# Input projection of a transformer layer: seven half-width products in place of eight, and the cache copies begun with the last column block

## What is computed

```
h  = rmsnorm(x, g_attn_norm)                  # 320 tokens x 2048
q, kc, vc, ks, vs, kw, vw, gt, u, v = split(h @ w_in)      # 2048 x 4656
q_rot, ks, kw = partial_rope(q), partial_rope(ks), partial_rope(kw)
gates = sigmoid(gt);  u = gelu(u);  v = rmsnorm(gelu(v), g_sgu_v)
kc_all, vc_all = compress(cached and new kc, vc; w_cmp_*1, w_cmp_*2, pe_cmp_*)
win_k_s = concat(cache_win_k, kw)[:, -wb:]    # and win_v_s: mostly a copy of the cache
mk, mv = rmsnorm(mem, g_mem_src) @ (w_mem_k, w_mem_v)
```

## Time and profile before

| | us |
|---|---|
| median of 3 runs (1652.16 to 1656.22) | 1654.53 |
| the profiled execution | 1652.59 |
| its span | 1650.8 |
| projection phase, first product to the next phase's first instruction | 80.58 to 424.04 |

### The profile page before, as it was taken

How to read it: one execution, slowest core, us unless ns; L and a number is a source line. 1 busy time by engine, 2 the same in 40 slices (tenths; PEclk the granted TensorE clock), 3 DMA queues, 4 the chain that set the end, 5 groups by cost and what they waited for, 6 DMA issues and landing times. The chain is left out here.

```text
span 1650.8 us, 19858 instructions
## 1 busy us (share of the span) xinstructions
PE 1443.3 (87%) x7384; PEld 794.2 (48%) x7385; DVE 387.3 (23%) x972; ACT 296.7 (18%) x667; POOL 83.5 (5%) x111
## 2 busy tenths in 40 slices
PE   7999999999999988878899999859879978699890
PEld 4444445556788756644444575533323333233330
DVE  3101010000365265466310212521100100101015
ACT  3000000011333234357100113201000000000001
POOL 0000000000200000000000000001001010010100
PEclk9999999999999689979899999969989988899895
DMA  9276224252242077500943222979998999979975
GB/s 357 104 303 254 103 99 139 99 173 103 103 153 65 22 220 229 158 12 1 340 135 110 94 102 103 388 276 401 392 415 307 414 404 388 416 309 414 414 299 195
DMA packets 112657, 371.89 MB, mean 225 GB/s; under 512 B 17331, under 2 KB 55259, under 8 KB 82919
## 3 DMA queue, kind: packets, MB, share of 16 engines
q1 hardware_dynamic: 106898, 334.88, 53.5%
q0 software_dynamic: 5552, 27.89, 4.9%
q10 hardware_dynamic: 144, 8.26, 1.2%
HBM read 394.60 MB, written 26.49 MB: 255 GB/s over the span
## 5 line engine op out<-in xcount | busy, mean ns | idle before, releaser
L2359 PE MATMUL bank<-ring,hT_e 128*64 x576 | 251.7, 595 | 8.2 <-DMA ring<-in_w_exp_up 6.8
L2360 PE MATMUL bank<-ring,hT_e 128*64 128x512 f32 x576 | 251.9, 595 | 0.0
L2376 PE MATMUL bank<-W,const 128*64 128x512 f32 x576 | 150.2, 677 | 53.1 <-DMA W<-in_w_exp_down 48.6
L2359 PEld LDWEIGHTS bank<-ring,hT_e 128*64 128x64 f32 x576 | 78.5, 138 | 167.7 <-issue 167.7
L490 PE MATMUL bank<-raw,hT 128*128 128x512 f32 (+1 forms) x320 | 131.6, 573 | 0.6 <-PEq L243 0.6
L490 PE MATMUL bank<-w_in,hT 128*128 128x512 f32 (+2 forms) x320 | 123.7, 547 | 0.0
L2376 PEld LDWEIGHTS bank<-W,const 128*64 128x64 f32 x576 | 45.0, 155 | 145.0 <-issue 100.5
L1715 PE MATMUL bank<-W,mixT 128*128 128x512 f32 x256 | 113.4, 603 | 1.6 <-DVE mixT L1950 1.6
L490 PEld LDWEIGHTS bank<-raw,hT 128*128 128x128 f32 x320 | 61.5, 193 | 67.5 <-issue 67.3
L490 PEld LDWEIGHTS bank<-w_in,hT 128*128 128x128 f32 x320 | 60.4, 190 | 61.0 <-issue 61.0
L1715 PEld LDWEIGHTS bank<-W,mixT 128*128 128x128 f32 x256 | 49.0, 193 | 63.5 <-issue 61.4
(11 more groups left out here) (403 smaller groups left out, 1782.5 us busy)
## 6 DMA issues: line engine op xcount, KB each, us to landing
ring<-in_w_exp_gate SPq DMA_DIRECT2D x80, 1024.0 KB
ring<-in_w_exp_up SPq DMA_DIRECT2D x72, 1024.0 KB
W<-in_w_exp_down SPq DMA_DIRECT2D x72, 1024.0 KB
raw<-in_w_in SPq DMA_DIRECT2D x3, 4096.0 KB
W<-in_w_out SPq DMA_DIRECT2D x3, 4096.0 KB, 13.3
w_in<-in_w_in SPq DMA_DIRECT2D x2, 4096.0 KB, 14.7
k_in<-in_cache_sel_k SPq DMA_DIRECT2D x64, 128.0 KB
v_in<-in_cache_sel_v SPq DMA_DIRECT2D x64, 128.0 KB, 3.5
```

The lines of the kernel that those rows point to most:

```text
L2359: pe.matmul(bank[4 + u][0:NS, :], hT[:, u, c, :], w_g[:, c, :], start=(c == 0), stop=(c == KC - 1))
L2360: mm = pe.matmul(bank[4 + u][UP, :], hT[:, u, c, :], w_u[:, c, :], start=(c == 0), stop=(c == KC - 1))
L2376: mm = pe.matmul(bank[2 * u + n // 2][lane, :], actT[:, q, :], w_d[:, q, 512 * n:512 * n + 512], start=(q == 0), stop=(q == 3))
```

## The change

- The 256 prompt tokens are taken as two tiles, the 2048 rows as two halves, the columns of a block as two halves, and the 2 x 2 x 2 products of halves become seven, each of eight matmuls 128 tokens by half the width. Four sums of token blocks are made once (`sum_tokens`), four sums of weight halves for each block (`sum_weights`, DVE, into the memory of `w_in1`). ACT keeps four partial results for a block, DVE adds up four outputs (`add_up`). The sample tokens are multiplied as before (`THIRD`).
- Nine column blocks: five of 512, and `V1, UV, GU, U1` of 524. One weight buffer, loaded in two halves of rows (`load_in`).
- The memory keys' transposes stand ahead of block `Q0`.
- The compression's weights are loaded after the last block's; `pe_terms` and `pe_sums` follow the last block; the gather starts after product 3 of the last block; ACT issues the cache copies at the start of its work on the last block.
- 0.8 MB of constants (the memory of the kept partial results) is loaded at the start of the compression phase instead of at the start.

```diff
+            Q0, KS, Q1, KW, KC_, V1, UV, GU, U1 = range(9)
...
+            JOBS = {FIRST: m_jobs, KS: q_jobs(0), KW: q_jobs(1), KC_: k_jobs}
+            THIRD, P1, P2, P5, P6, P3, P7, P4 = range(1, 9)
...
+                    def load(n):
+                        sp.wait_ge(ready, made(n - 1, P1))
+                        sp.wait_ge(w_summed, added(n - 1, T3))
+                        load_in(sp, 0, *COLS[n])
+                        sp.wait_ge(ready, made(n - 1, P3))
+                        sp.wait_ge(w_summed, added(n - 1, T4))
+                        load_in(sp, 1, *COLS[n])
...
-                        if n == V1:
+                        if n == U1:
+                            sp.wait_ge(v_squared, TILES)
                             for u, kind in enumerate("kv"):
                                 sp.dma_start(w1[:, u, :, :], A[f"w_cmp_{kind}1"][0].rearrange("(m p) h -> p m h", p=P)).then_inc(cw_loaded, 16)
...
-                    pool.wait_ge(ready[0], TILES * (NT_IN // 2))
+                    pool.wait_ge(ready, made(NT_IN - 1, P3))
+                    pool.wait_ge(w_summed, added(NT_IN - 1, T4))
                     for turn in range(2):
                         gather_cmp(pool, turn)
...
+                        def product(to, left, right, start=True):
+                            for c in range(8):
+                                mm = pe.matmul(to, left(c), right(c), start=(start and c == 0), stop=(c == 7), skip_group_check=True)
+                            mm.then_inc(ready, 1)
...
+                        pe.wait_ge(kept, copied_out(n, K_THIRD))
+                        pe.wait_ge(w_summed, added(n, T1))
+                        product(b, lambda c: s1[:, c // 4, c % 4, :], lambda c: w_sum[:, 0, c, 0:half])
+                        pe.wait_ge(kept, copied_out(n, K_P1))
+                        pe.wait_ge(w_summed, added(n, T2))
+                        product(a, lambda c: s2[:, c // 4, c % 4, :], lambda c: w_sum[:, 1, c, 0:half], start=False)
...
+                    turn_blocks(FIRST)
                     for n in range(NT_IN):
                         multiply(n)
                         turn_blocks(n)
-                        if n == UV:
-                            pe_terms()
-                        if n == GU:
-                            pe_sums()
+                    pe_terms()
+                    pe_sums()
                     pe_columns()
...
                 def _(act):
                     own = act_steps.on(act)
                     act.wait_ge(blank_q, 2)
-                    act.wait_ge(ready[0], 1)
-                    for cache, dst in (("cache_win_k", "win_k_s"), ("cache_win_v", "win_v_s")):
...
+                    copy_jobs(act, act.copy, 0, FIRST)
+                    for n in range(NT_IN):
+                        if n == U1:
+                            for cache, dst in (("cache_win_k", "win_k_s"), ("cache_win_v", "win_v_s")):
+                                act.dma_start(out[dst][0, :, 0:WIN - NT].rearrange("b (s t) g d -> b s (t g d)", s=NT),
+                                              A[cache][0, :, NT:WIN].rearrange("b (s t) g d -> b s (t g d)", s=NT)).then_inc(window_out, 16)
+                        take(n)
+                        if n == GU:
+                            act.wait_ge(v_scaled, 1)
+                            act.activation(vms[:, :], vms[:, :], ACT.Sqrt).then_inc(v_rooted, 1)
+                        if n > KC_:
+                            finish(n)
                         copy_jobs(act, act.copy, 0, n)
...
+                        dve.tensor_tensor(t(0), part(0, 1), part(0, 0), ALU.subtract).then_inc(w_summed, 1)
...
+                        if n:
+                            dve.wait_ge(ready, made(n - 1, P4))
+                        dve.wait_ge(w_summed, added(n, T2))
+                        dve.tensor_tensor(t(3), t(1), part(1, 0), ALU.subtract).then_inc(w_summed, 1)
...
+                    for n in range(NT_IN):
+                        sum_weights(n)
+                        if 1 <= n <= KC_ + 1:
+                            take(n - 1)
+                        if n - 1 in JOBS and n - 1 != FIRST:
+                            copy_jobs(dve, dve.tensor_copy, 1, n - 1)
...
+                        add_up(n)
```

More of the change, by code:

```diff
@@ L263, in _ @@
                     sp.wait_ge(mem_made, 2)
[L264 removed]
+                    for v in range(2):
+                        load_in(sp, v, 0, 512)
                     sp.wait_ge(const_loaded, 16 * 5)
@@ L478, in multiply @@
                         half = width // 2
-                        pe.wait_ge(loaded[u], n // 2 * 16 + 16)
-                        if n >= 2:
[L481 to L493, removed]
-                                    mm = pe.matmul(bank[4 * u + r][64 * h:64 * h + 64, 0:half], hT[:, c, r * P:r * P + NS], part,
-                                                   start=(c == 0), stop=(c == KC - 1))
-                            mm.then_inc(ready[u], 1)
@@ new lines, in multiply @@
+                        for c in range(KC):
+                            if c % 8 == 0:
+                                pe.wait_ge(w_in_loaded[c // 8], 16 * n + 16)
+                            for h in range(2):
+                                mm = pe.matmul(b[64 * h:64 * h + 64, :], hT[:, c, 2 * P:2 * P + NS], w[:, c, h * half:(h + 1) * half],
+                                               start=(c == 0), stop=(c == KC - 1))
+                        mm.then_inc(ready, 1)
+                        if n >= 2:
+                            pe.wait_ge(kept, copied_out(n - 2, K_U3))
@@ L565, in _ @@
-                    for n in range(NT_IN):
-                        take(n)
+                        u, width = n % 2, COLS[n][1]
+                        half = width // 2
+                        a, b = (bank[4 * u + k][:, 0:half] for k in range(2))
+                        gelu = n > KC_ and n != GU
+                        act.wait_ge(ready, made(n, THIRD))
+                        if n == Q1:
+                            act.wait_ge(turned, J_BEFORE[KS + 1])
+                            act.wait_ge(roped, KS + 1)
@@ new lines, in take @@
+                        for h in range(2):
+                            to, shaped = half_of(n, 2, h)
+                            of = shaped(b[64 * h:64 * h + 64, :])
+                            ins = act.activation(to, of, ACT.Gelu_apprx_tanh) if gelu else act.copy(to, of)
+                        ins.then_inc(kept, 1)
+                        act.wait_ge(ready, made(n, P1))
+                        if n:
+                            act.wait_ge(summed, added(n - 1, C21))
+                        act.copy(kept_p1[:, 0:half], a).then_inc(kept, 1)
```

242 lines of the change are left out of this document (156 added, 86 removed).

## The result

The changed kernel takes **1669.48 us** (median of 8 runs, 1663.97 to 1672.76) against 1654.2 us (8 runs, 1652.16 to 1658.32): a ratio of 1.0089, 95% interval 1.007 to 1.0108. It is slower by 15 us. The profiled execution has a span of 1668.2 us, 17.4 more than before.

What follows compares the result with a forecast made beforehand. PE's own work was taken to set the phase's time, plus whatever makes PE wait. Terms gave -9.8 us, then +28 for the copies and +2 for the clock: +20.2, 1672.8 profiled, 1674 forecast, range 1664 to 1683.

Steps and rivals of the forecast that it cites:

- forecast case: Whole kernel: slower at 1674 us, range 1664 to 1683, the new last wait outweighing the phase's gain; chance 0.68.
- Products: PE's column blocks: seven 256-column products instead of eight half products, blocks of 31.4 and 32.2 us, saving 30.6 us.
- rival 3: Late halves: six blocks wait up to 0.8 us each for weights, 5 us in all, total 1679; chance 0.05.
- Turns: After KS and KW, transposes wait behind DVE's weight sums: 14.6 us each; with the memory's transposes, +17.0 us together.
- Clock: PE standing some 10 us twice: 2.8 us charged for each, less the 2.8 that goes: +2.8 us.
- Tail without the wait: Last block's end to next phase: 10.1 us, with DVE's output and copy ahead of the sums adding 1.0.
- Copies: Before `pe_terms`: cache copies hold up the compression's weights, so PE stands 28 us, 22 to 33.
- Sums at the low clock: After the last wait, PE's small sums start at the low clock: +2 us, 0 to 2.8.
- Rival 1: Weights get through in the gaps, only the gather is late: +11 us, total 1655, no change; chance 0.14.
- Rival 2: Copies do not hold other queues: no wait before `pe_terms`, -9.8 us, 1644, faster; chance 0.13.

Runs made afterwards that it cites:

- order experiment: Changed kernel, but after blocks KS and KW DVE rotates and copies the transposed jobs out before making the four weight sums: 1654.79 us, ratio 0.9989.
- sixteen-part run: Changed kernel with each cache copy written with an outer dimension of 16 instead of 8, same bytes, place and issue time: 1660.41 us, ratio 1.0023.
- the kernel with the new order, the weights first and sixteen parts: Changed kernel, DVE rotating and copying before its weight sums after KS and KW, compression's weights issued before the last half load, copies in sixteen parts: 1626.99 us, ratio 0.9827.

## Why the prediction was right

The forecast case came in: 1674 was predicted, 1669.5 measured, in the range of 1664 to 1683 that the case had for itself, and the wait that it named is the one that decides. By its own steps, in us of the profiled execution:

- **Products:** blocks of 31.4 and 32.2 predicted, 31.43 and 32.18 measured. The saving of 30.6 stands. No block starts late, so rival 3 falls.
- **Turns:** 14.6 each predicted, 15.1 measured; +7.8 and +9.05 instead of +7.3 and +8.6. PE stood for 10.65, ended by the copy into `qrT`, as written. With the 1.0 for the memory's transposes: +17.8 against +17.0. The order experiment shows the cause.
- **Clock:** +2.8 predicted, +0.4 measured (1.94 and 1.30 lost, 2.8 no longer). The step was wrong in taking 2.8 us for each stand; see the last section.
- **Tail without the wait:** 10.1 predicted, 10.2 in the five kernels without a wait there.
- **Copies:** 28 predicted (22 to 33), 24.6 measured. The mechanism is shown by the two directions of it: away from the copies the wait is gone (27.3 us between the last block and the next phase); put beside anything else (the first blocks' weights, the gather of the kernel before) they stall that by 24 and 12 us. The order of events is the predicted one, copies, gather, weights: the semaphore was reckoned for S+59 and came at S+56.8 (426.87), and the remaining 1.2 of the 3.4 too many is that 28 was taken where the count gave E+26.8. I had read the one-for-one from 8 packets; it holds in the finer rows above (8 beside 8) and in the sixteen-part run (96 beside 95). It is not the whole: from 382 to 384.5 SP's queue passed 80 packets beside 8 of the copies', 72 of them under 512 bytes, and again from 389.5 to 392 and from 394.5 to 397. Why the small ones go in bursts no run shows.
- **Sums at the low clock:** +2 predicted, +2.7 measured (9.81 against 7.15).
- **Rival 1** was hidden under the forecast: without the weights' wait the gather's costs 11.8. **Rival 2** did not come in: the copies went out before the weights were through, at S+0.7, a little ahead of the S+1 to S+5.4 reckoned.

These terms sum to -30.6 + 17.8 + 0.4 + 1.0 + 24.6 + 2.7 = +15.9, where the phase grew by 15.7. The forecast of 20.2 was 4.3 too high, 3.4 of it in the copies' term and 2.4 in the clock, less what the turns and the sums had more. Two further differences, neither of them forecast, almost cancel: the rest of the program grew by 1.7, and the median lies 0.6 below the profiled execution where the prediction put it 1.9 above.

On the packet size, the Trainium skill's "DMA: Bandwidth & Descriptors" (queues, rings and completion order) speaks of typically 9 to 17 descriptors a packet. Here SP's packets beside the copies are 0.20 MB in 96, about 2 KB, or four rows of 512 bytes; the measurement decides, and rival 1, to which the page's packets pointed, did not come in by itself. The same page (the section on why a semaphore goes up by 16) says that a DMA uses the largest number of engines up to 16 that divides the outer dimension of both its sides. The trace agrees: cut in 8, the copies held 44.8% of the engines' time from 382 to 390; cut in 16, 90.4% from 375 to 385, and they were through in 31 us where they had taken some 46.

## What to carry to other kernels

A bulk copy "in the background" is free only beside transfers with slack: look up what is on the queues in its 30 to 50 us, above all small packets and indirect gathers that somebody waits for, and put those ahead of it or it elsewhere. When a wait is removed, look for the next one under it (here 24.6 us of weights hid 11.8 of the gather), and try the repairs together. Work put ahead of a copy on DVE, however well hidden in the middle of a block, is paid in full where PE waits for that copy at the block's end.

## What had not been expected of the hardware

**ACT's queue issues DMAs while earlier work of ACT is still to come.** The copies stand in ACT's stream behind two table loads and a Gelu; the first was issued at 370.71, the Gelu ran at 372.22. What held it back was the wait ahead, on `v_scaled`: the activation with that wait began at 370.70. In the kernel before with the copies late it is the same: issues at 386.75 and 388.10, two activations that stand before both at 388.02 and 390.45. So in these kernels an issue "after" a piece of work was not delayed by it.

**What the clock costs behind a stand does not follow the stand's length.** After the turn at `KS` the next 64 products (7.13 us at full speed) took 9.07 in the changed kernel, where PE had stood for 10.65 us, and 9.91 in the kernel with the new order, the weights first and sixteen parts, where it had stood for 1.82. The granted clock there, in that last kernel (columns: PE, PEld, DVE, ACT, POOL busy; clock; DMA share; GB/s):

```profile
144.00:150.00 6.00, 3.56 (x26) 2.46 (x26) 4.05 (x17) 1.54 (x3) 0.00 (x0) 0.85 0.02 4
150.00:156.00 6.00, 6.00 (x36) 3.43 (x34) 5.87 (x3) 0.00 (x0) 0.00 (x0) 0.58 0.00 0
```

In windows of 1 and 2 us it was full until 148, 0.63 from 148 to 149, 0.50 (the 1.2 GHz level) until 154, 0.73 from 154 to 156 and full again after: it fell about a microsecond before the turn's end at 149.40. In the changed kernel it was 0.93 from 148 to 150, 0.50 until 162, 0.65 from 162 to 164: it fell in the stand, where a low clock costs nothing, and came back 4 us into the block, against nearly 6 here. That is why the longer stand lost less.

The kernel before lost nothing after `KS` and 2.8 after `KW`; with its copies moved to the attention phase, and not one instruction of that stretch changed, it lost 2.3 after `KS` and 2.6 after `KW` (27.73 at full speed):

```profile
156.99 30.00 PE L490 MATMUL bank<-raw,hT 128*128 128x512 f32 x64
...
234.76 30.37 PE L490 MATMUL bank<-raw,hT 128*128 128x512 f32 x64
```

Over all traces a turn cost between 0 and 2.8 us. For some kernels it differs with the execution: in the changed kernel and its variants with the old order the 64 products after `KS` took 8.47 to 9.92 us, with a stand of 10.65 or 10.66 in each. The three with the new order agree within 0.04 (9.91 to 9.95). So a single trace doesn't price it. The Trainium skill's "TensorE: Matmul & The Clock Gate" (what's actually happening) has the like for the first matmuls of a kernel: how many of them run slow differs from run to run. The rows here show such a spread in the middle of one.
